# Three-unit dilated attention: the transposes of the probabilities follow two steps behind a pair's last scores instead of three

## What is computed

```python
for g, (w, d) in enumerate(DIL_PATTERNS):
    ...
    o, lse = banded_attention(to_res(q[:, :, g])[:, :, :, None], to_res(k[:, :, g]), to_res(v[:, :, g]),
                              w // d + 1, cols, dist_scale=d)
    ...
wts = jax.nn.softmax(jnp.stack(lses), axis=0)
return jnp.sum(wts[..., None] * jnp.stack(outs), axis=0)
```

## Time and profile before

| | |
|---|---|
| median of 3 runs | 1713.15 us (1712.02 to 1715.89) |
| the profiled execution's own time | 1711.66 us |
| its span | 1709.9 us |
| PE busy | 1634.5 us (96%) |
| DVE busy | 1132.4 us (66%) |
| ACT busy | 937.7 us (55%) |
| POOL busy | 119.0 us (7%) |
| mean granted clock of TensorE | 0.983 |

### The profile page before, as it was taken

How to read it: one execution, slowest core, us unless ns; L and a number is a source line. 1 busy time by engine, 2 the same in 40 slices (tenths; PEclk the granted TensorE clock), 3 DMA queues, 4 the chain that set the end, 5 groups by cost and what they waited for, 6 DMA issues and landing times.

```text
span 1709.9 us, 24655 instructions
## 1 busy us (share of the span) xinstructions
PE 1634.5 (96%) x8997; PEld 1376.9 (81%) x8997; DVE 1132.4 (66%) x1808; ACT 937.7 (55%) x1520; POOL 119.0 (7%) x172
## 2 busy tenths in 40 slices
PE   8998999989899998999999799999999998899999
PEld 7886888888678886888887578888888887578887
DVE  5955765677675567766667466667666673667665
ACT  5554655557565555555566565556555554665554
POOL 0601000000000000000003300000000010410000
PEclk9999999999999998999999999999999997999999
DMA  9332464574345644656464045565555573026652
GB/s 318 124 123 99 148 199 169 203 251 135 108 144 176 218 150 148 199 170 212 173 242 148 1 140 189 187 198 171 181 187 194 199 250 124 1 79 217 199 169 99
DMA packets 216786, 283.91 MB, mean 166 GB/s; under 512 B 8328, under 2 KB 152712, under 8 KB 216712
## 3 DMA queue, kind: packets, MB, share of 16 engines
q1 hardware_dynamic: 216712, 282.93, 49.5%
HBM read 281.81 MB, written 1.09 MB: 165 GB/s over the span
## 4 chain that ended last, share of the span: by engine, by line
PE 85%; DVE 8%; ACT 4%; issue 1%; SPq 1%; POOL 0%; DMA 0%; ACTq 0%; DVEq 0%
PE banks L966 29%; PE banks L967 15%; PE banks L739 12%; PE banks L740 11%; PE banks L741 11%; DVE ring_lo L348 1%; PE banks L1288 1%; PE banks L1321 1%; PE banks L1301 1%; ACT ring_hi L340 1%; PE banks L1651 1%; SPq L446 1%; DVE stats L580 1%; PE banks L2910 1%; PE banks L670 1%
## 5 line engine op out<-in xcount | busy, mean ns | idle before, releaser
L966 PE MATMUL banks<-act_both,ring_hi 128*128 128x512 f32 x2112 | 751.2, 397 | 3.3 <-DVE act_both L612 1.6
L967 PE MATMUL banks<-act_both,ring_lo 128*128 128x256 f32 x2112 | 592.4, 281 | 0.0
L966 PEld LDWEIGHTS banks<-act_both,ring_hi 128*128 128x128 f32 x2112 | 397.3, 188 | 100.4 <-issue 4.4
L967 PEld LDWEIGHTS banks<-act_both,ring_lo 128*128 128x128 f32 x2112 | 397.4, 188 | 5.0
L1082 DVE TENSOR_TENSOR ring_lo<-weight_slots,ring_hi 128x1024 fp32r<-128x1024 f32 x240 | 283.3, 1222 | 62.5 <-ACT ring_hi L1037 62.2
L348 DVE TENSOR_TENSOR ring_lo<-weight_slots,ring_hi 128x1024 fp32r<-128x1024 f32 (+4 forms) x150 | 182.0, 1226 | 98.1 <-ACT ring_hi L340 95.0
L1037 ACT ACTIVATE ring_hi<-weight_slots 128x1024 fp32r<-128x1024 f32 x240 | 239.2, 1044 | 1.1 <-DMA weight_slots<-in_ffn_w 1.1
L1051 ACT ACTIVATE normed<-banks 128x512 f32<-128x512 f32 x132 | 78.9, 597 | 289.4 <-PE banks L967 289.4
L739 PE MATMUL banks<-ffn_down_hi,ffn_hidden_hi 128*128 128x512 f32 x528 | 207.5, 393 | 0.4
L740 PE MATMUL banks<-ffn_down_lo,ffn_hidden_hi 128*128 128x512 f32 x528 | 206.8, 392 | 0.0
L741 PE MATMUL banks<-ffn_down_hi,ffn_hidden_lo 128*128 128x512 f32 x528 | 205.8, 390 | 0.0
(11 more groups left out here) (372 smaller groups left out, 1916.2 us busy)
## 6 DMA issues: line engine op xcount, KB each, us to landing
weight_slots<-in_ffn_w SPq DMA_DIRECT2D x44, 1024.0 KB, 6.5
weight_slots<-in_ffn_w_gate SPq DMA_DIRECT2D x44, 1024.0 KB, 5.4
weight_slots<-in_ffn_w_up SPq DMA_DIRECT2D x44, 1024.0 KB, 8.0
weight_slots<-in_ffn_w_down SPq DMA_DIRECT2D x88, 512.0 KB, 8.4
weight_slots<-in_ffn_w SPq DMA_DIRECT2D x44, 512.0 KB, 8.3
weight_slots<-in_ev_w_in SPq DMA_DIRECT2D x6, 2048.0 KB, 12.2
weight_slots<-in_od_w_in SPq DMA_DIRECT2D x5, 2048.0 KB, 11.4
weight_slots<-in_ab_w_in SPq DMA_DIRECT2D x4, 2048.0 KB, 11.3
```

Source lines behind the costliest of these rows:

```text
L966: pe.matmul(bank, k.hi(n)[:, q, :], k.act_both[:, q], start=q == 0, stop=False, skip_group_check=True)
L967: return pe.matmul(bank[:, 0:S], k.lo(n)[:, q, :], k.act_hi[:, q, :], start=False, stop=q == KD - 1, skip_group_check=True)
```

## The change

Two lines change. The lag of an attention with more than one unit goes from 3 to 2, so that all its flips, the value products behind them and DVE's reciprocals ahead of them come one step earlier, and the stage has 16 steps instead of 17. Output parts 2 and 3 go from steps 10 and 12 to 9 and 11; the later splits of the output weights and of the next layer's first ones go from steps 11, 13 and 15 to 10, 12 and 14. Part 1 stays in step 8.

```diff
-        self.LAG = 2 if self.G == 1 else 3
+        self.LAG = 2
...
-        attend(k, block, Chain(mla, dil, 4), out, {6: [0], 8: [1], 10: [2], 12: [3]}, {1: 3, 3: 4, 11: 5, 13: 6, 15: 8},
+        attend(k, block, Chain(mla, dil, 4), out, {6: [0], 8: [1], 9: [2], 11: [3]}, {1: 3, 3: 4, 10: 5, 12: 6, 14: 8},
                side=ab, tile_waits=tile_waits)
```

## The result

| | before | changed |
|---|---|---|
| median | 1713.15 us (3 runs, 1712.02 to 1715.89) | 1721.66 us (3 runs, 1721.64 to 1724.00) |
| ratio, 95% interval | | 1.0045 [1.0025, 1.0064] |
| span of the profiled execution | 1709.9 us | 1719.9 us |
| scores 3 start | 964.65 | 970.18 |
| first flip 0 starts | 970.61 | 975.07 |

It is slower. Measured once more with 12 runs beside 29 of the kernel before, the ratio was 1.0036 [1.0025, 1.0048], so that the size is 6 to 8 us, 0.4%.

A forecast was written before the change was run, and what follows sets the result against it. PE, with 85% of the span, was taken to bound the kernel. Order 3.4 plus clock 1.5 + 1.5 gave 6.4 us: 1718.1 on the profiled 1711.66, 1719.5 on the median; forecast 1718.5 us, range 1714.5 to 1721.0.

The forecast's parts named there:

- The order's term: Three-unit attention: earlier flips make PE wait 4.5 us, second exponentials start 5.0 us later, 1.5 given back: +3.4 us.
- Rival (d): ACT's queue at step 9: not slower, the shorter end wins, 1710.2 us if second exponentials start as now; chance 0.05.
- The clock's term: PE behind its two new waits, 4.5 and 2.7 us: low clock costs 1.5 us each, bounds nothing and 3.0.
- rival (c): Behind the first gap the low stretch lasts 6.9 us: 1719.6 us on the profile, 1721 on the median; chance 0.09.
- rival (b): Only one of PE's two gaps lowers the clock: +4.9 us, 1716.6 us; chance 0.22.
- my 0.44: Price of half clock with PE at work: of 3.4 us at that rate 1.5 us are lost.
- The splits and loads at nothing: Out-weight splits and the following layer's weights, asked for some 3 us later: no cost, or once up to 3 us.

The follow-up runs named there:

- the profile with filler: Changed kernel plus idle matmuls nobody reads, 14 ahead of duo 0's first flip and 8 ahead of duo 3's: stage 31.83 us, ratio to before 1.0010.
- the second profile: The changed kernel profiled and run once more, nothing altered: stage 34.23 us, 6.9 us of it at the low clock, ratio to before 1.0036.
- tables alone: Kernel before, lag kept at 3, with the new tables of output parts and splits: stage 33.60 us, ratio to before 1.0033.
- one copy on DVE: Kernel before with the second copy of flip 1 done by DVE instead of ACT: stage 26.94 us, ratio to before 0.9979.
- lag alone: Lag 2 with the old tables of output parts and splits: stage 34.27 us, ratio to before 1.0033.
- exponentials ahead of the copy: Changed kernel with ACT's second pair of exponentials ahead of its copy of flip 1: stage 37.62 us, ratio to before 1.0054.

## Why the prediction was right, and where not

**The order's term, +3.4 us: right step by step.** At full clock the profile with filler has the first flip 5.47 us after scores 3 (worked out 5.40), the second exponentials 13.68 us after (13.77), and from there to the last parts 18.15 us (18.13). The wait added on PE, its 7.3 us of own work ahead of the second flip 1, ACT's exponentials behind the copy, and the step given back at the end were all where the working had them. Rival (d), the shorter end, did not come: the exponentials would have had to start 10.3 us after scores 3.

**The clock's term, +1.5 and +1.5: right in kind, too small in size.** Half clock at the first wait came in both profiles of this kernel; it lasted 6.9 us, the end of the range in rival (c), not the 3.4 us that I took from the row at 165.7 us. At the second wait it came in one of the two, so the second profile is rival (b). The price can be read flip by flip against the profile with filler. From the first flip 0 to the second flip 1 PE takes 7.30 us at full clock (974.62 to 981.92), 10.31 in the first profile and 9.85 in the second: 3.0 and 2.5 us lost. From flip 3 to the tail it is 4.51 us at full clock and 7.01 in the first profile: 2.5 lost. Part of each low stretch fell into the wait, where it costs nothing; per us at half clock with PE at work the price is 0.46 us in all three cases (6.53, 5.59 and 5.43 us of it), close to my 0.44. So the price was right and the length wrong. The stage grew by a little less than these losses, since the low clock ahead of it held scores 3 back more than the exponentials, and the first flip came 4.89 and 5.33 us after scores 3 instead of 5.47.

The rule that I quoted from the Trainium skill ("TensorE: Matmul & The Clock Gate", "Why this matters for your kernels"), that idle gaps between bursts of matmuls put the array back to its half rate, held at the first wait, of 3.96 and 4.40 us. But the waits of 2.52 us ahead of the stage, which I took as safe from one row at 1.00, had half clock at 958 to 968 us here, and again in the second profile.

**The number: too low.** 1718.5 us was forecast and 1721.66 measured as the median of three, 0.66 us above the range's upper end of 1721.0. The rise is 8.5 us between the two medians, 7.7 by the ratio and 6.2 by the ratio of the later measurement; forecast were 5.35 on the median and 6.4 by the sum. Two steps made it too low. The mis-sized term of the sum is the clock's: 1.5 + 1.5 us, where the profiled execution lost 3.0 + 2.5, so that the stage grew by 8.3 us and not by 6.4. In the second profile it grew by 5.8, since the second wait passed at full clock. The other step is the 1.0 us that I took off the sum on the median (1719.5), because the kernel before might lose the clock in this stage too: its profile shows none, and its gain from filler is only a hint. What the first two profiled executions differ by outside the stage, +5.5 and -3.8 us, was in no term. That 1713.15 was a low draw is possible, since three later measurements of the kernel before gave 1714.6 to 1716.8; but they were taken on other occasions, and it is not shown.

**The splits and loads at nothing: right as far as is seen.** ACT's waiting for a DMA at L1037 was 0.3 us in the changed kernel against 1.1, and the rest of the program behind the stage took 713.0 us against 716.8:

```profile
L1037 ACT ACTIVATE ring_hi<-weight_slots 128x1024 fp32r<-128x1024 f32 x240 | 239.3, 1045 | 0.3 <-DMA weight_slots<-in_ffn_w 0.3
```

## What to carry to other kernels

When an operation that must wait is moved earlier in an engine's own order, everything behind it inherits the wait; count what used to stand ahead of it and filled the time, here 3.7 us of scores and an output part. The wait goes on into another engine's in-order queue when a long block there (5.4 us of exponentials) stands behind a short copy fed by the moved work; that order alone cost 0.9 us here. Look first for the idle engine: one copy handed to DVE got the 1.5 us that the earlier flips were to bring.

## What was not expected of the hardware

A wait of 2.5 us on PE can be passed at full clock or not by the same instructions: behind the wait of 2.52 us ahead of scores 3 the clock stood at 1.00 in the profile of the kernel before and at half in both of the changed kernel. Of all profiles without filler in that wait four had 1.00 behind it (before, changed + filler in two waits, tables alone, one copy on DVE), and the other six had half clock behind it or behind the wait of 1.64 us that follows.

Low stretches in the stage lasted 6.8 to 6.9 us in eight cases, in or just behind waits of 4 us, of 3.06 us and of 2.5 us alike, and 10.3 us in one, behind two waits of 2.48 and 1.36 us. A first wait of 4.0 to 4.4 us without filler had half clock behind it in all four profiles that have it (changed, changed again, lag alone, exponentials ahead of the copy); with 3.39 us of idle matmuls in it, it had 1.00 in both. In the changed kernel filler was worth 0.24 to 0.35%, in the kernel before 0.15%. All four profiles with filler are at 1.00 throughout, but so are the kernel before and the version with one copy on DVE, so that for lag 3 the profiles do not show what filler does.
